# Feed-forward weights loaded in halves, and a second set of block products in the fourth quarter

## What is computed

```python
D_FF = 5632
def swiglu(x, w_gate, w_up, w_down):
    return (jax.nn.silu(x @ w_gate) * (x @ w_up)) @ w_down
```

## Time and profile before

| | us |
|---|---|
| runs of the kernel before | 2803.5, 2804.95, 2806.48 |
| median | 2804.95 |
| span of the profiled execution (first to last instruction) | 2803.9 |
| TensorE busy | 2789.1 |
| VectorE busy | 2219.1 |
| ScalarE busy | 1485.1 |

### The profile page before, as it was taken

The page is one execution under the profiler, slowest core; times in us unless marked ns, Lnnn a source line. Parts: engine busy times, 40 slices in busy tenths (PEclk is TensorE's granted clock), DMA queues, the critical chain, the costliest instruction groups (busy, mean ns, idle before and its releaser), DMA issues.

```text
span 2803.9 us, 34346 instructions
## 1 busy us (share of the span) xinstructions
PE 2789.1 (99%) x13154; PEld 2329.8 (83%) x13154; DVE 2219.1 (79%) x2554; ACT 1485.1 (53%) x1747; POOL 14.5 (1%) x20
## 2 busy tenths in 40 slices
PE   9999999999999999999999999999999999999998
PEld 8888888888898888888888888888888888888887
DVE  6869757865565888889888877687799888889885
ACT  5544545554544555555455555755655555555564
POOL 0000000000000000000000000000000000000000
PEclk9999999999999999999999999999999999999999
DMA  7546355555545555655655558543665656565654
GB/s 250 202 155 199 112 182 190 186 189 180 165 150 197 196 193 197 206 199 199 202 196 194 196 165 270 177 160 125 204 200 189 203 187 208 197 204 198 204 187 158
DMA packets 276010, 530.71 MB, mean 189 GB/s; under 512 B 8769, under 2 KB 32465, under 8 KB 275393
## 3 DMA queue, kind: packets, MB, share of 16 engines
q1 hardware_dynamic: 274864, 527.01, 56.6%
q0 software_dynamic: 752, 2.04, 0.2%
q10 hardware_dynamic: 288, 0.20, 0.0%
HBM read 527.12 MB, written 2.10 MB: 189 GB/s over the span
## 4 chain that ended last, share of the span: by engine, by line
PE 97%; DVE 1%; DMA 0%; ACT 0%; issue 0%; SPq 0%; DVEq 0%; ACTq 0%
PE ps L817 19%; PE ps L818 19%; PE ps L820 17%; PE ps L1373 10%; PE ps L1375 9%; PE ps L1374 9%; PE ps L826 2%; PE ps L902 1%; PE ps L901 1%; PE ps L900 1%; PE ps L845 1%; PE ps L846 1%; PE ps L850 1%; PE ps L1081 1%; PE ps L1367 1%; PE ps L1061 1%
## 5 line engine op out<-in xcount | busy, mean ns | idle before, releaser
L2450 DVE TENSOR_TENSOR w_lo<-raw,w_hi 128x2048 fp32r<-128x2048 f32 (+4 forms) x301 | 663.0, 2206 | 193.9 <-ACT w_hi L1683 193.1
L1683 ACT ACTIVATE w_hi<-raw 128x2048 fp32r<-128x2048 f32 (+4 forms) x301 | 555.1, 1849 | 259.5 <-DMA raw<-in_ff_w_down 107.4
L817 PE MATMUL ps<-w_hi,x_hi 128*128 128x512 f32 (+4 forms) x1760 | 679.1, 386 | 1.7 <-ACT z L1716 0.7
L818 PE MATMUL ps<-w_lo,x_hi 128*128 128x512 f32 (+4 forms) x1760 | 669.5, 380 | 0.0
L820 PE MATMUL ps<-w_hi,x_lo 128*128 128x512 f32 (+4 forms) x1536 | 582.7, 379 | 0.0
L817 PEld LDWEIGHTS ps<-w_hi,x_hi 128*128 128x128 f32 x1760 | 330.7, 188 | 62.6 <-issue 2.3
L818 PEld LDWEIGHTS ps<-w_lo,x_hi 128*128 128x128 f32 x1760 | 330.9, 188 | 58.6
L820 PEld LDWEIGHTS ps<-w_hi,x_lo 128*128 128x128 f32 x1536 | 288.4, 188 | 53.3
L2217 ACT ACTIVATE w_hi<-raw 128x1024 fp32r<-128x1024 f32 x156 | 164.9, 1061 | 278.4 <-DMA raw<-in_ff_w_up 144.7
L1373 PE MATMUL ps<-w_hi,x_hi 128*128 128x512 f32 x780 | 305.4, 392 | 0.1
L1375 PE MATMUL ps<-w_hi,x_lo 128*128 128x512 f32 x780 | 303.8, 389 | 0.0
(11 more groups left out here) (486 smaller groups left out, 4019.4 us busy)
## 6 DMA issues: line engine op xcount, KB each, us to landing
raw<-in_w_in SPq DMA_DIRECT2D x139, 1024.0 KB, 5.1
raw<-in_ff_w_gate SPq DMA_DIRECT2D x88, 1024.0 KB, 5.2
raw<-in_ff_w_up SPq DMA_DIRECT2D x88, 1024.0 KB, 5.3
raw<-in_ff_w_down SPq DMA_DIRECT2D x88, 1024.0 KB, 5.1
raw<-in_w_out SPq DMA_DIRECT2D x45, 1024.0 KB, 5.2
raw<-in_w_ple_gate SPq DMA_DIRECT2D x16, 1024.0 KB, 5.0
raw<-in_w_in SPq DMA_DIRECT2D x8, 696.0 KB, 4.3
raw<-in_w_in SPq DMA_DIRECT2D x8, 520.0 KB, 3.8
```

The lines of the kernel that those rows point to most:

```text
L817: nc.tensor.matmul(o, x[0][:, k0 + c, s], hi[:, c, 0:width], start=first and c == 0, stop=False)
L818: nc.tensor.matmul(o, x[0][:, k0 + c, s], lo[:, c, 0:width], start=False, stop=False)
L1683: nc.scalar.activation(landed_part(w_hi, u, j), landed_part(raw, u, j), ACT.Copy).then_inc(hi_ready, 1)
L2450: V.tensor_tensor(landed_part(w_lo, u, j), landed_part(raw, u, j), landed_part(w_hi, u, j).bitcast(F32), ALU.subtract).then_inc(parts_read ...
```

## The change

- Weights of the feed-forward, from those that block 1 uses to those of block 9, are loaded as two transfers of 512 KB a unit, each half (chunks 0 and 1, chunks 2 and 3) with its own release: first halves when TensorE has counted `firsts_used`, second ones by `parts_used` as before. First halves land in semaphores of their own. The units of block 0 and the very last four stay whole.
- In blocks 1 to 9 the fourth quarter (p = 3, `DOUBLE`) takes both halves of its chunks by seven products, so 14 products and not 15. The order on all three engines is written anew, in smaller steps; block 0 keeps the old order of its products.
- Sums of weights go to two buffers in turn (`sums_place`).
- The second set needs four more sums of tiles of x. VectorE makes them in block 0 (`half_x_sums`, 10 instructions of 128x128), ScalarE their high parts, and VectorE their low parts (`half_x_sums_lo`, 128x512) behind the last `down_added` of block 0. TensorE waits for them ahead of block 1.
- `down` takes banks 6, 4, 6, 4, so that its units 2 and 3 wait for the sums added for units 0 and 1 (`added`). The transposed hidden values go to banks 0 and 1, and not to 6 and 7. `silu` is written in place.
- VectorE adds the gates (`gates_added`) before it splits unit 1 of w_down, splits units 2 and 3 at once, and makes the hidden values after that.
- `load_gain` is issued ahead of the last four units.

The core of the diff; ScalarE's order follows VectorE's and is left out but for the next block's first quarter:

```diff
+    DOUBLE = 3
+    GROUPS = [(p, 0) for p in SUMMED] + [(DOUBLE, 1)]
+    NG = len(GROUPS)
+    NG_ALL = len(SUMMED_FIRST) + NG * (FB - 2)
+    HALF_LOADS = 12 * (FB - 2)
...
         def down_bank(i, j):
-            if isinstance(i, int) and i >= FB - 2:
-                return (6, 4, 2, 6)[j] if i == FB - 2 else 4 + 2 * (j % 2)
-            return 6 - 2 * j
-        def summed_of(i):
...
+        def sums_place(i, p, h):
+            return 0 if isinstance(i, int) and i == 0 else GROUPS.index((p, h)) % 2
+        def sums_since(i, p, h):
+            return 1 if isinstance(i, int) and i == 0 or (p, h) == (0, 0) else 3 if p == 1 else 2
...
+                def load_half(u, j, h, src):
+                    if h:
+                        sp.wait_ge(parts_used, u - (RAW - 1))
+                    else:
+                        sp.wait_ge(firsts_used, first_halves_used(no, u0, u - RAW))
+                    sp.dma_start(slot(j, UC, BW)[:, 2 * h:2 * h + 2],
+                                 src.rearrange("(k p) n -> p k n", p=P)).then_inc((first_landed, raw_landed)[h][j], 16)
+                def gate_and_up_halves(u, i):
+                    for j in range(4):
+                        by_unit, by_half = ((0, 0), (0, 1), (1, 0), (1, 1)), ((0, 0), (1, 0), (0, 1), (1, 1))
+                        for m, h in by_half if j == DOUBLE else by_unit:
+                            k = j * BW + h * BW // 2
+                            load_half(u + (2 * j + m), (2 * j + m) % RAW, h,
+                                      (gate, up)[m][k:k + BW // 2, bass.ds(i * BW, BW)])
+                def down4_halves(u, i):
+                    for j in range(4):
+                        for h in range(2):
+                            load_half(u + j, j, h, down[bass.ds(i * BW + h * BW // 2, BW // 2), j * BW:(j + 1) * BW])
...
                 gate_up(u0, 0)
-                then()
-                with sp.Fori(0, FB - 1) as i:
-                    gate_and_up(i * 12 + (u0 + 8), i + 1)
-                    down4(i * 12 + (u0 + 16), i)
+                gate_and_up(u0 + 8, 1)
+                down4(u0 + 16, 0)
+                with sp.Fori(0, FB - 2) as i:
+                    gate_and_up_halves(i * 12 + (u0 + 20), i + 2)
+                    down4_halves(i * 12 + (u0 + 28), i + 1)
+                sp.wait_ge(ws_used, sums_before(no, 0) + NG_ALL)
+                load_gain(row)
                 down4(u0 + 12 * FB - 4, FB - 1)
...
+                    if release and c == n // 2 - 1:
+                        m.then_inc(firsts_used, 1)
...
+                    products = {0: 2 * 3 + NG, 1: 2 * 3, 2: 2 * 3 + NG, 3: 2 * 3 + NG, 4: NG, 5: NG, 6: NG, 7: NG}
+                    def product_of(bank, held, moving):
+                        k = done.get(bank, 0)
+                        done[bank] = k + 1
+                        return three(bank, held, moving, k == 0, k + 1 == products[bank])
...
+                    def gate_first(p):
+                        pe.wait_ge(parts_ready, u + (2 * p + 1))
+                        product_of(6, x(p, 0, 0), weights(p, 0, 0))
+                        product_of(2, x(p, 1, 0), weights(p, 0, 1)).then_inc(firsts_used, 1)
...
+                    def sums(p, h=0):
+                        g = n + GROUPS.index((p, h))
+                        pe.wait_ge(ws_ready, g * 2 + 1)
+                        product_of(4, xsum(p, h, 0), sum_of(p, h, 0))
+                        product_of(5, xsum(p, h, 1), sum_of(p, h, 1))
+                        pe.wait_ge(ws_ready, g * 2 + 2)
+                        product_of(3, x(p, 2 * h + 1, 1), sum_of(p, h, 2)).then_inc(ws_used, 1)
+                    def gate_second(p):
+                        pe.wait_ge(plain_ready, (s + p) * 2 + 1)
+                        product_of(6, x(p, 2, 0), weights(p, 0, 2))
+                        product_of(2, x(p, 3, 0), weights(p, 0, 3)).then_inc(parts_used, 1)
+                    def ups_of_both(p):
+                        pe.wait_ge(parts_ready, u + (2 * p + 2))
+                        product_of(7, xsum(p, 0, 2), weights(p, 1, 0))
+                        pe.wait_ge(plain_ready, (s + p) * 2 + 2)
+                        product_of(7, xsum(p, 1, 2), weights(p, 1, 2)).then_inc(shared_done, 1)
+                        product_of(0, xsum(p, 0, 3), weights(p, 1, 1)).then_inc(firsts_used, 1)
+                        product_of(0, xsum(p, 1, 3), weights(p, 1, 3)).then_inc(parts_used, 1)
+                    gate_first(0)
+                    turn_hidden(i, 0)
+                    plain(0, 0)
+                    pe.wait_ge(added, i * 4 + a0)
+                    sums(0)
+                    pe.wait_ge(st_done, i * 2 + (turned_before[hname] + 2))
+                    up_first(0)
+                    plain(0, 1)
+                    plain(1, 0)
+                    gate_first(1)
+                    up_first(1)
+                    sums(1)
+                    plain(1, 1)
+                    gate_first(2)
+                    sums(2)
+                    plain(2, 0)
+                    up_first(2)
+                    plain(2, 1)
+                    sums(3)
+                    gate_second(3)
+                    gate_first(3)
+                    sums(3, 1)
+                    ups_of_both(3)
...
-                        bank = down_bank(i, j)
                         if j == 0:
                             pe.wait_ge(rest_summed, i * 2 + (2 * shared_before(no) + 2))
-                        if bank == 4 and j < 2:
+                        elif j == 1:
                             pe.wait_ge(rest_done, c)
-                        if bank == 2:
-                            pe.wait_ge(gates_summed, c)
-                        elif bank == 0:
-                            pe.wait_ge(ups_summed, c)
-                        elif j >= 2:
+                        else:
                             pe.wait_ge(added, i * 4 + (a0 + j - 1))
                         if last and j == 3:
                             last()
-                        unit(u + j, j, 0, UC, BW, down_bank(i, j), True, True, (h_hi, h_lo))
+                        unit(u + j, j, 0, UC, BW, down_bank(i, j), True, True, (h_hi, h_lo), release=True)
...
                 all_drained(pe, b)
                 product(u0 + 4, 0)
-                block_of_hidden(0)
+                first_block_of_hidden()
+                pe.wait_ge(half_xs_ready, no + 1)
                 with pe.Fori(0, FB - 3) as i:
...
+                def next_first_quarter(u, i):
+                    gate_second_hi(u, 0, i)
+                    up_second_hi(u, 0, i)
+                    gate_first_hi(u, 0, i)
+                    first_sums_hi(i, 0)
+                    third_sum_hi(i, 0)
+                    up_first_hi(u, 0, i)
...
+                def half_x_sums():
+                    c0 = DOUBLE * UC + 2
+                    a = {(c, tt): [x[:, c0 + c, tt * P:(tt + 1) * P].bitcast(F32) for x in (x_hi, x_lo)]
+                         for c in range(2) for tt in range(2)}
+                    low = half_xs_low[:]
+                    of = lambda m: half_xs[:, m]
+                    def done(ins, step):
+                        ins.then_inc(half_xs_made, 1)
+                        dve.wait_ge(half_xs_made, 6 * no + step)
+                    V.tensor_tensor(of(0), a[0, 1][0], a[1, 1][0], ALU.add)
+                    V.tensor_tensor(of(2), a[0, 0][0], a[0, 1][0], ALU.subtract)
+                    done(V.tensor_tensor(low, a[0, 1][1], a[1, 1][1], ALU.add), 1)
+                    done(V.tensor_tensor(of(0), of(0), low, ALU.add), 2)
+                    V.tensor_tensor(of(1), of(0), a[0, 0][0], ALU.subtract)
+                    done(V.tensor_tensor(low, a[0, 0][1], a[0, 1][1], ALU.subtract), 3)
+                    V.tensor_tensor(of(2), of(2), low, ALU.add)
+                    done(V.tensor_tensor(of(1), of(1), a[0, 0][1], ALU.subtract), 4)
+                    done(V.tensor_tensor(of(3), a[1, 0][0], of(1), ALU.subtract), 5)
+                    done(V.tensor_tensor(of(3), of(3), a[1, 0][1], ALU.add), 6)
+                def half_x_sums_lo():
+                    dve.wait_ge(half_xs_hi_ready, no + 1)
+                    V.tensor_tensor(half_xs_lo[:], half_xs[:], half_xs_hi[:].bitcast(F32),
+                                    ALU.subtract).then_inc(half_xs_ready, 1)
...
+                def first_sum(u, p, i, h=0):
+                    n, j = group(i, p, h), 2 * p % RAW
+                    landed(u + 2 * p, j, h, i)
+                    landed(u + (2 * p + 1), j + 1, h, i)
+                    since = sums_since(i, p, h)
+                    if not isinstance(n, int) or n >= since:
+                        dve.wait_ge(ws_used, n - (since - 1))
+                    V.tensor_tensor(ff_ws[sums_place(i, p, h)][:, 0], raw_half(p, 1, h)[:, 0], raw_half(p, 0, h)[:, 0],
...
+                    first_sum(u, 1, i)
+                    second_sums(1, i)
+                    gate_second_lo(1, i)
+                    third_sum(1, i)
```

(113 more changed lines are left out.)

367 lines of the change are left out of this document (229 added, 138 removed).

## The result

| | before | after |
|---|---|---|
| median, us | 2804.73 | 2810.61 |
| lowest to highest | 2803.5 to 2809.29 | 2808.42 to 2813.54 |
| span of the profiled execution | 2803.9 | 2810.2 |
| mean granted clock | 0.999 | 0.996 |
| matmul instructions | 13154 | 13100 |

The account below looks back on a forecast made before the run. TensorE, busy without a gap in the loop, was taken as the bound: 2803.9 - 12.2 (fewer matmuls) + 12.9 (block 0 waits) = 2804.6 us profiled, 2805.6 as median, with a range of 2800 to 2815.

Parts of the forecast that it names:

- rival 1: The clock falls in the long gap at block 0: one fall 2808, two 2810.2 us; chance 0.22.
- the main sum: Whole kernel: 2803.9 - 12.2 + 12.9 = 2804.6 us for a profiled execution, 2805.6 for the median.
- The term removed: Fourth quarter of blocks 1 to 9, both feed-forwards: 14 products instead of 15, 12.2 us less, a pass of 62.7.
- The loop costs nothing: In blocks 1 to 9 VectorE keeps up, busy 60.8 of 62.7 us; deadlines hold by 0.4 to 1 us.
- The chain itself: VectorE's loop steps from quarter 2's sums (12.4 us) to w_down unit 0's low part (38.6), without a pause.
- another deadline of the prediction: In the loop, the low part of quarter 3's second gate half is done at 32.5 us against 33.5.
- Rival 2: The loop loses because halves land late and w_down is released late: 0.6 us a block, 10.8, 2816; chance 0.2.
- Halves and gain load: Half loads land in 3.7 us, and the gain load moves ahead of the last four units; neither costs time.
- Block 0: TensorE waits for VectorE 1.9 us before w_down unit 3 and 4.5 before block 1: +12.9 us over both feed-forwards.
- Rival 3: Block 0's gap is much smaller: sums of x fit VectorE's 2.75 us idle, forced 4.4 stay; 2801.5; chance 0.08.
- The clock: A fall some 3.6 us after TensorE goes idle, against a 4.5 us gap at block 0; 2.3 us lost each.

Follow-up runs that it names:

- e3_both: The changed kernel with TensorE's wait for the new sums moved inside block 1 and the sums of x made ahead of block 0's quarter 3: 2793.53 us, ratio 0.996.
- e7: e3_both with three more VectorE operations a block in blocks 1 to 9, ahead of quarter 3's sums: 2817.09 us, ratio 1.0044.
- e6: e3_both with one more VectorE operation a block in blocks 1 to 9, ahead of quarter 3's sums: 2796.32 us, ratio 0.9972.
- e2: The changed kernel with the ten operations for the new sums of x moved ahead of block 0's quarter 3, TensorE's wait unmoved: 2807.37 us, ratio 1.0008.
- e4: The changed kernel with both block 0 waits kept but filled with small unread TensorE products: 2805.74 us, ratio 1.0004.
- e1: The changed kernel with TensorE's wait for the new sums moved from ahead of block 1 to their first use inside it: 2798.57 us, ratio 0.9979.

## Why the prediction was right or wrong

The time lies inside the range of 2800 to 2815, 5.0 us above the forecast of 2805.6. The forecast was no difference beyond 0.2% at 0.66; the change is slower by 0.21%, which had 0.27. The time fits the price of rival 1 with two falls, 2810.2, and not the main sum; that the range holds it is owed to that rival.

**The term removed: right.** 54 matmuls fewer, and a pass 0.7 us shorter in the mean. e3_both, where nothing else is left, is 10.9 us under before.

**The loop costs nothing: right, but with less to spare than was worked out.** No wait of TensorE in it. VectorE's busy time came out at 60.37 for the forecast's 60.8. The chain itself, in VectorE's timeline of block 1:

```profile
1047.62 0.69 DVE L3516 TENSOR_TENSOR z<-raw 128x512 f32<-128x512 f32 x1 [1.62 <-DMA raw<-in_ff_w_up]
...
1057.06 0.69 DVE L3516 TENSOR_TENSOR z<-raw 128x512 f32<-128x512 f32 x1 [0.66 <-DMA raw<-in_ff_w_up]
...
1074.50 0.68 DVE L3576 TENSOR_TENSOR z<-z,ps 128x512 f32<-128x512 f32 x1
1075.38 0.69 DVE L3583 TENSOR_TENSOR z<-z,ps 128x512 f32<-128x512 f32 x1 [0.20 <-PE ps L1427]
```

The sums of quarter 2 wait 1.62 us for the up half and those of quarter 3 0.66, where I had VectorE busy without a pause from the first on; the first rest starts at 1074.50, the second waits 0.20 us for TensorE. So `rests` weren't late. What is tightest is another deadline of the prediction, quarter 3's second gate half, in the timelines of VectorE and then of TensorE:

```profile
1066.02 2.35 DVE L3544 TENSOR_TENSOR w_lo<-raw,w_hi 128x1024 fp32r<-128x1024 f32 x2
```

```profile
1068.99 0.39 PE L1425 MATMUL ps<-w_hi,x_hi 128*128 128x512 f32 x1
```

Its low part is done at 1068.37 and TensorE takes it at 1068.99: 0.6 us, and 0.4 in the same place of e3_both, where the prediction had 1.0. This is where TensorE waits in e7, and e6 and e7 measure the slack as 0.5. Rival 2, that the loop loses, is out for this change. Its price was too low: the prediction had 0.9 us free before a delay counts, so e7's 1.8 us would have cost 0.9 a block, and they cost 1.3.

**Halves and gain load: right.** Gate and up land in 3.7 us; in the feed-forwards TensorE has no wait for a load. The DMA engines' share grew by 2.4 points, as the batching rule of the Trainium skill ("DMA: Bandwidth & Descriptors", section "Bandwidth") would have it, but it changed no wait. The halves of w_down land in 4.6 us and not in 3.7, and no wait of TensorE rests on them.

**Block 0: right.** Forecast 1.9 and 4.5 us idle, measured 1.8 and 4.7 (longest); VectorE was to finish at 1033.4 and did at 1033.5. TensorE resumed at 1033.9, 0.4 us behind that, at a low clock. Rival 3, that the sums fit into VectorE's idle time, is out: they fit only when moved, in e2 and e3.

**The clock: this is the step that failed.** The sum took the granted clock as full throughout, so slow matmuls stood in it at nothing, and put a fall into rival 1, at 0.22, with "one fall 2808, two 2810.2". In the profiled execution it fell three times. The granted clock in windows of one microsecond around the gaps of the kernel after (columns as above):

```profile
1032.00:1033.00 1.00, 0.00 (x0) 0.00 (x0) 1.00 (x2) 0.00 (x0) 0.00 (x0) 1.00 0.29 111
1033.00:1034.00 1.00, 0.07 (x1) 0.08 (x1) 0.49 (x1) 0.00 (x0) 0.00 (x0) 0.75 0.00 0
1034.00:1035.00 1.00, 1.00 (x3) 0.81 (x4) 0.00 (x0) 0.00 (x0) 0.00 (x0) 0.50 0.00 0
1037.00:1038.00 1.00, 1.00 (x10) 0.96 (x9) 0.00 (x0) 0.58 (x2) 0.00 (x0) 1.00 0.00 0
2098.00:2099.00 1.00, 0.84 (x3) 0.68 (x4) 1.00 (x3) 0.26 (x1) 0.00 (x0) 0.73 0.75 260
2108.00:2109.00 1.00, 0.00 (x0) 0.00 (x0) 1.00 (x2) 0.00 (x0) 0.00 (x0) 0.85 0.59 227
2109.00:2110.00 1.00, 0.00 (x0) 0.00 (x0) 0.63 (x2) 0.00 (x0) 0.00 (x0) 0.50 0.00 0
2116.00:2117.00 1.00, 1.00 (x6) 0.84 (x5) 0.97 (x3) 0.27 (x1) 0.00 (x0) 1.00 0.21 80
```

A mean of 0.75 is half a microsecond at 1.00 and half at 0.50. So in the first feed-forward the clock falls near 1033.5, 0.4 us before TensorE resumes, and is full again at 1037. In the second it falls behind the short gap near 2098.5, recovers, and falls again near 2108.7, within the long gap. The timeline of TensorE there:

```profile
2098.16 0.56 PE L867 MATMUL ps<-w_hi,h_hi 128*128 128x512 f32 x1 [1.80 <-DVE z L3627]
2098.52 0.63 PE L868 MATMUL ps<-w_lo,h_hi 128*128 128x512 f32 x1
...
2101.51 0.57 PE L870 MATMUL ps<-w_hi,h_lo 128*128 128x512 f32 x1
...
2105.11 0.39 PE L870 MATMUL ps<-w_hi,h_lo 128*128 128x512 f32 x1
2110.06 0.79 PE L1425 MATMUL ps<-w_hi,x_hi 128*128 128x512 f32 x1 [4.56 <-DVE half_xs_lo L3484]
...
2112.78 1.91 PE L1419 MATMUL ps<-ident,z 128*128 128x128 f32 x8
...
2115.34 0.49 PE L1427 MATMUL ps<-w_hi,x_lo 128*128 128x512 f32 x1
```

From 2098.16 to 2101.91 nine matmuls take 3.75 us, where behind the same gap in the first feed-forward nine take some 2.15: 1.6 us lost. From 2110.06 on six matmuls lose 1.4, the transposes 0.8 (1.56 against 0.79) and the next three 0.6: 2.8. In the first feed-forward it is 1.4 + 0.1 = 1.5. Together 5.9 us by the timeline of an execution 1.4 us above the median, 5.4 by TensorE's busy time, 4.9 between the medians by e4. With the last the sum is 2805.6 + 4.9 = 2810.5, and 2810.61 was measured; that says no more than that e4, without the slow work, came out at the forecast. The evidence stood in the prediction itself: a fall 3.6 us after the last matmul, and a gap of 4.5. I gave the only row that there was a chance of 0.22, since its margin was 0.9 us; it deserved the greater part, and the price in the sum. That the clock can also fall behind a gap of 1.8 us no row of before showed.

The page "TensorE: Matmul & The Clock Gate" of the Trainium skill (Part 1) has the monitor run free of the kernel and the point of a change of clock vary with it. The traces agree: in the two long gaps the fall came 4.2 and 3.2 us after the end of the last matmul, and the same short gap was followed by a fall in one feed-forward and by none in the other, nor in the trace of e1.

## What to carry to other kernels

Put a wait where its data are first used, not ahead of the loop, above all on the engine that bounds the time: here that alone was worth 12 us, twice what the whole change lost. When new one-time work is placed on a second engine, follow that engine's timeline to the next thing that the bounding engine needs from it, and place the work in a stretch where the trace shows it idle. Price a gap of TensorE at its length and the slow matmuls behind it, which took 1.5 to 3.1 us more behind each of the four traced gaps of 4.6 to 4.7 us.

## What was unexpected of the hardware

- The granted clock can fall behind 1.8 us of idleness: at 2098 it was 0.73 in the mean of a microsecond, which puts the fall near 2098.5, after TensorE had resumed (it was idle from 2096.4 to 2098.2). The same gap 1075 us earlier, and both in the trace of e1, had no fall behind them.
- The way back took 3.0 us of work in one place and 5.5 in another, behind gaps of nearly the same length (4.66 and 4.56 us): 1.5 and 2.8 us lost. In e2, behind gaps of 4.66 and 4.56 us, it took 6.0 and 6.2: 3.0 and 3.1 us lost.
- TensorE's first matmul behind the long gap started 0.4 us after VectorE's last operation had ended, where behind the short gap it was 0.05 (1023.49 to 1023.54). The low clock isn't the cause: in e4, at full clock and with the small products in the wait, it is 0.4 as well (1033.22 to 1033.66). At the long gap TensorE also enters its loop; whether that is it wasn't tested.
